# Packing the weight units and moving each low half behind its high half

## The chip, the cores and the metric

One NeuronCore of one Trainium2 chip runs the whole program. The metric is the device time of one execution in microseconds (us); of the kernel before three executions were timed, and their median is 2285.76 us (2285.3 to 2287.43).

## What is computed

A forward pass of 256 tokens of width 1024, in float32, through two blocks of two layers each. Cut to what carries the time:

```python
# first block, twice: layer norm, "0.5 * swiglu" with d_ff 4096, a mixer, and again a swiglu
x = layer_norm(alpha * x + 0.5 * swiglu(x, w_ff1_in, w_ff1_out), ...)     # (silu(gate) * up) @ w_out
x = layer_norm(alpha * x + hybrid_mixer(x, ...), ...)    # delta rule + two attentions, gates, w_out
x = layer_norm(alpha * x + 0.5 * swiglu(x, w_ff2_in, w_ff2_out), ...)
# second block, twice: a mixer (convolution and pooling; then sparse attention), and a swiglu, d_ff 2816
x = x + mixer(rms_norm(x, norm_mix))
x = x + swiglu_2(rms_norm(x, norm_ffn), ffn_gate, ffn_up, ffn_down)
```

Nearly all bytes and nearly all multiplications belong to products of the activations with weight matrices that are read once each.

## The kernel before

Each weight matrix is cut into *units* of at most 128 x 1040 numbers. There are 732 of them, taken in one fixed order. A unit goes through four steps, each on an engine of its own:

- SyncE loads it into one of four raw buffers `RW0` to `RW3` (`load`, L2316), which it may do once VectorE has finished with the unit four places earlier.
- ScalarE rounds it to the short format that TensorE multiplies fast and writes the *high half* `WH` (`cut`, L983; in the units marked `seven` L980 and L981).
- VectorE subtracts and writes the rest, the *low half* `WL` (`cut`, L1364; in `seven` units L1357 and L1360).
- TensorE multiplies. The activations are split in the same way (`XT` holds high and low in one row of 512 numbers, `HTH` and `HTL` are the hidden layer of a swiglu), and a product is the sum of three: high by high, high by low, low by high.

The program is written by a `Walk` that is run once for each engine; five `Program` classes issue the instructions of their engine and wait on semaphores. Order, waits and buffers come from the `Walk` and do not depend on addresses.

A pair (`WH[n]`, `WL[n]`) is a *slot*. There are six of them (`SPL = 6`); two more (`more_slots`, `WH6`, `WL6`, `WH7`, `WL7`) lie in the scratch area `SCR` and are lent for part of the time, and two (`xt_slots`) lie in `XT` itself, which is free while the second product of a large swiglu runs. A slot is placed by `Unit.place`, and `Unit.part` says where in it (and in the raw buffer) the unit's numbers lie. The forms of TensorE's work that the prediction speaks of are these:

- `tile_part` (L560, L559, L562): the gate and up products of a swiglu. The units are four blocks of 256 columns (nk = 4). The weights are the *stationary* operand, which is loaded into the array in its own instruction (PEld), and the activations stream through: for each block and column tile one matmul of 512 columns (high weights by high and low activations at once, L560), and one of 256 (low weights by high activations, L559; L562 in the first block).
- `rows_part` (L466, L467, L468, called through `mm3`): the down products and most projections. The units are two blocks of 512 columns (nk = 2). Activations are stationary, and the weights stream: `WH`, `WL`, `WH`, 512 columns each.
- `cols_part` (L463, L464, L465): some projections, with two blocks, weights stationary and 256 streaming columns.
- `seven_part` (L541, L542, L543): part of the down products, in matmuls of 256 columns, weights streaming.

In `Unit.part` a unit of more than two blocks lies packed at the front of its slot, 1024 numbers without a gap. A unit of one or two blocks keeps the slot's own rows, so its second block begins 520 numbers (2080 bytes) behind the first. In `XT` the rows are 512 numbers long, so a unit that is placed there has its second block 2048 bytes behind the first and its low half 4096 bytes behind its high half.

The tiles are given out one after the other in the order of the declarations. With distances counted in bytes from the start of `XT` (16384 bytes long) the raw buffers begin at 16384 and are 4160 bytes each, `WH[n]` begins at 33024 + 4160 n, `WL[n]` 24960 bytes behind `WH[n]`, then come `ST` (256 bytes) and the area `SCR` at 83200. All that lies in `SCR` (`HTH`, `HTL`, the lent slots, the mixers' tiles) is given by offsets from its start.

Of the kernel before, what the change touches and what calls it, by code (L numbers as in the profile page):

```python
# [11 lines left out]
R = mybir.dt.float32r  # L12

P = 128
# [8 lines left out]

KU = 2
UW = 520
RAW = 4
SPL = 6
LEAD = 4
# [103 lines left out]
class Signals:  # L132
# [15 lines left out]
    ]  # L148
    LOADS = (["d_raw%d" % n for n in range(RAW)] + ["d_x0", "d_x1", "d_ident", "d_const", "d_gb0", "d_gb1", "d_rg"]
             + ["d_small%d" % n for n in range(10)] + ["d_stage%d" % n for n in range(3)]  # L150
# [29 lines left out]
class Unit:  # L180
# [14 lines left out]
        self.h2, self.l2 = [v.rearrange("p k n -> p (k n)")[:, 0:768] for v in slot]  # L195

    def part(self, v):
        if self.nk <= KU:
            return v[:, 0:self.nk, 0:self.src.shape[2]]
        flat = v.rearrange("p k n -> p (k n)")  # L200
        return flat[:, 0:self.nk * self.src.shape[2]].rearrange("p (k n) -> p k n", k=self.nk)


class Tiles:


    def __init__(self, nc, a, ctx):
        self.a = a

        def sb(name, shape, dt=F):  # L210
            return ctx.enter_context(nc.sbuf_tensor(name, shape, dt))
# [6 lines left out]
        self.XT = sb("XT", [P, 8, 2 * T], R)  # L218
        self.XTH, self.XTL = self.XT[:, :, 0:T], self.XT[:, :, T:2 * T]
        self.RW = [sb(f"RW{n}", [P, KU, UW]) for n in range(RAW)]  # L220
        self.WH = [sb(f"WH{n}", [P, KU, UW], R) for n in range(SPL)]
        self.WL = [sb(f"WL{n}", [P, KU, UW], R) for n in range(SPL)]
        self.ST = sb("ST", [P, 64])
        self.PS = ctx.enter_context(nc.psum_tensor("PS", [P, 8, 512], F))
        room = 229344 - nc.sbuf_base - 96
# [6 lines left out]
        def at(kb, name, shape, dt=F):  # L232
            n = 4
            for s in shape[1:]:
                n *= s
            off = int(kb * K)
            assert off + n <= room, (name, off + n, room)
            tile = nc.alloc_sbuf_tensor_at(name, shape, dt, offset=base + off)
            return tile[tuple(slice(None) for _ in shape)]
# [8 lines left out]
        self.slots = [(self.WH[n], self.WL[n]) for n in range(SPL)]  # L248
        self.more_slots = [tuple(at(72 + 8.125 * n + 4.0625 * m, f"W{'HL'[m]}{SPL + n}", [P, KU, UW], R) for m in range(2))
                           for n in range(2)]  # L250
# [204 lines left out]
class TensorProgram(Program):  # L455
# [470 lines left out]
    def odd_out(self, I, b):  # L926
        k = self.k
        t = I.t
        self.wait_ge("odd_a", (I.id, "pt", t))
        self.wait_ge("odd_a", ("vv", 1))  # L930
        self.emptied(b)
        self.wait_ge("odd_a", ("vcb", 3))
        parts = [(x, kt) for x in range(2) for kt in range(t + 1)] + [None]
        for part, n in ([(part, n) for part in parts for n in range(2)] if t else
                        [(part, n) for n in range(2) for part in parts]):
            h = I.hs[n]
            if part is None:
                self.wait_ge("odd_a", "ptc")
                v, p = k.VCB[:, h // 2, h // 4, :], k.PTC[:, 2 * t + h % 2, :]
            else:  # L940
                v, p = k.VV[:, part[0], part[1], 64 * (h // 4):64 * (h // 4) + 64], I.pt[:, tsl(I.block(part[0], n, part[1]))]
            ins = self.e.matmul(I.out(b, n), v, p, start=part == (0, 0), stop=part is None, skip_group_check=True)
        ins.then_inc(*self.s["mm"].up(b.full))
# [18 lines left out]
class ScalarProgram(Program):  # L962
# [10 lines left out]
    def cut(self, u):  # L973
        k = self.k
        raw = u.part(k.RW[u.n % RAW])
        self.wait_ge(f"d_raw{u.n % RAW}", u.n)
        self.wait_each(u.after)
# [39 lines left out]
    def half_sum(self, f, seq, sl, n, part, j, b, free):  # L1017
        self.wait_each(free)
        self.wait_ge("mm", b.full)
        self.e.activation(f[2 + part][:, n, j * T:j * T + T], self.k.PS[:, b.n, 0:T],  # L1020
                          ACT.Copy).then_inc(*self.s["ffn_a"].up((seq, sl, n, part, j)))
# [305 lines left out]
class VectorProgram(Program):  # L1327
# [8 lines left out]
    def mix(self, u, mixed, free):  # L1336

        k = self.k
        raw = u.part(k.RW[u.n % RAW])
        b11, b12, b21, b22 = [raw[:, m, c] for m in range(2) for c in (slice(0, 256), slice(256, 512))]  # L1340
        t2, t3, t4 = [mixed[:, m, :] for m in range(3)]
        self.wait_ge(f"d_raw{u.n % RAW}", u.n)
        self.wait_each(free)
# [2199 lines left out]
```

## Time and profile before

| | |
|---|---|
| time, median of 3 | 2285.76 us (2285.3 to 2287.43) |
| the profiled execution, first to last instruction | 2283.4 us |
| TensorE matmuls, busy | 2250.3 us (99%), 14127 instructions |
| TensorE weight loads, busy | 1927.4 us (84%) |
| VectorE, busy | 1624.1 us (71%) |
| ScalarE, busy | 1193.1 us (52%) |
| GpSimd, busy | 128.4 us (6%) |
| DMA, mean rate | 179 GB/s |

The profile is of one execution. Times in its rows are us from the first instruction unless marked ns; a row `PS<-XT,WH` is an instruction that writes PSUM from the tiles XT and WH, the streaming and the stationary operand being named in no fixed order. Successive matmuls overlap, and the end of one is modelled, so the duration of a matmul is longer than the distance to the next one's start; both rise and fall together, since what one matmul takes longer delays the next start by as much.

### The profile page before, as it was taken

What the parts mean: (1) busy time and instruction counts of PE and PEld (TensorE: products, weight loads), DVE (VectorE), ACT (ScalarE), POOL (GpSimd) and SP (SyncE); (2) the same over time, 40 slices, a digit from 0 to 9 for tenths busy, and PEclk for the clock granted to TensorE, in tenths of its full rate; (3) what the DMA queues carried; (4) which work ended last, traced back from release to release, by engine and by line L of the source; (5) the groups of instructions that cost most, each with busy time, mean ns of one, the idle gap of its engine ahead of it and who ended that gap; (6) DMA issues with size and microseconds to landing.
All of it is one profiled execution on the core that took longest, in us unless ns stands there. A gap on an engine that the chain in (4) does not pass through costs nothing.

```text
span 2283.4 us, 34563 instructions
## 1 busy us (share of the span) xinstructions
PE 2250.3 (99%) x14127; PEld 1927.4 (84%) x14127; DVE 1624.1 (71%) x2491; ACT 1193.1 (52%) x1872; POOL 128.4 (6%) x185
## 2 busy tenths in 40 slices
PE   8999999999999999999999999999999999989999
PEld 7888899888888888888898877888878888867887
DVE  5777768857777777768668667776877778666776
ACT  5555446534555546555356444655444555545553
POOL 2100010120000000000100110000000000420000
PEclk9999999999999999999999999999999999999999
DMA  6765564435565556655554336665644666643654
GB/s 225 224 190 192 189 222 122 140 121 177 192 191 190 183 193 203 190 191 198 191 183 139 127 115 209 199 192 173 212 161 166 207 191 194 196 130 104 200 179 148
DMA packets 283567, 408.17 MB, mean 179 GB/s; under 512 B 13700, under 2 KB 170688, under 8 KB 283152
## 3 DMA queue, kind: packets, MB, share of 16 engines
q1 hardware_dynamic: 275600, 380.91, 51.9%
q0 software_dynamic: 7808, 25.04, 3.8%
q8 instruction: 112, 1.84, 0.3%
q14 instruction: 47, 0.39, 0.1%
HBM read 403.98 MB, written 1.91 MB: 178 GB/s over the span
## 4 chain that ended last, share of the span: by engine, by line
PE 89%; DVE 7%; ACT 3%; issue 1%; DMA 1%; SPq 0%; DVEq 0%; ACTq 0%
PE PS L560 24%; PE PS L466 12%; PE PS L468 12%; PE PS L467 12%; PE PS L559 11%; PE PS L463 2%; PE PS L465 2%; PE PS L464 2%; DVE WL L1364 2%; PE PS L562 2%; PE PS L483 1%; PE PS L543 1%; PE PS L541 1%; PE PS L542 1%; DVE QX L1659 1%
## 5 line engine op out<-in xcount | busy, mean ns | idle before, releaser
L1364 DVE TENSOR_TENSOR WL<-RW,WH 128x1024 fp32r<-128x1024 f32 x682 | 809.0, 1220 | 177.7 <-ACT WH L983 173.3
L560 PE MATMUL PS<-XT,WH 128*128 128x512 f32 x2368 | 808.0, 394 | 0.0
L983 ACT ACTIVATE WH<-RW 128x1024 fp32r<-128x1024 f32 x682 | 685.2, 1042 | 232.7 <-PE PS L468 62.9
L559 PE MATMUL PS<-XT,WL 128*128 128x256 f32 x2072 | 580.8, 280 | 0.0
L560 PEld LDWEIGHTS PS<-XT,WH 128*128 128x128 f32 x2368 | 425.2, 188 | 76.1
L559 PEld LDWEIGHTS PS<-XT,WL 128*128 128x128 f32 x2072 | 389.9, 188 | 13.4
L466 PE MATMUL PS<-WH,XT 128*128 128x512 f32 (+4 forms) x640 | 249.3, 390 | 3.8 <-DVE WL L1364 2.9
L468 PE MATMUL PS<-WH,XT 128*128 128x512 f32 (+4 forms) x640 | 240.5, 376 | 0.0
L467 PE MATMUL PS<-WL,XT 128*128 128x512 f32 (+4 forms) x640 | 240.0, 375 | 0.0
L466 PE MATMUL PS<-WH,HTH 128*128 128x512 f32 x488 | 192.6, 395 | 0.0
L468 PE MATMUL PS<-WH,HTL 128*128 128x512 f32 x488 | 192.2, 394 | 0.0
L467 PE MATMUL PS<-WL,HTH 128*128 128x512 f32 x488 | 191.4, 392 | 0.0
L463 PE MATMUL PS<-XT,WH 128*128 128x256 f32 x560 | 164.1, 293 | 2.3 <-DVE Z L1546 1.0
L464 PE MATMUL PS<-XT,WL 128*128 128x256 f32 x560 | 158.1, 282 | 0.0
L465 PE MATMUL PS<-XT,WH 128*128 128x256 f32 x560 | 158.1, 282 | 0.0
L1434 DVE TENSOR_TENSOR HM<-PS,HM 128x256 f32<-128x256 f32 x148 | 62.4, 422 | 133.1 <-ACT HM L1020 133.1
L466 PEld LDWEIGHTS PS<-WH,XT 128*128 128x128 f32 x640 | 121.2, 189 | 36.2 <-DVE XT L1375 8.6
L1020 ACT ACTIVATE HM<-PS 128x256 f32<-128x256 f32 x148 | 56.9, 384 | 169.6 <-PE PS L560 166.4
L468 PEld LDWEIGHTS PS<-WH,XT 128*128 128x128 f32 x640 | 121.1, 189 | 23.8
L467 PEld LDWEIGHTS PS<-WL,XT 128*128 128x128 f32 x640 | 121.4, 190 | 19.7
L1020 ACT ACTIVATE SG<-PS 128x256 f32<-128x256 f32 x148 | 54.2, 381 | 122.2 <-PE PS L560 120.8
L463 PEld LDWEIGHTS PS<-XT,WH 128*128 128x128 f32 x560 | 106.7, 190 | 6.9 <-issue 2.8
(500 smaller groups left out, 3221.8 us busy)
## 6 DMA issues: line engine op xcount, KB each, us to landing
RW<-in_w_ff_in SPq DMA_DIRECT2D x256, 512.0 KB, 4.4
RW<-in_w_ff_out SPq DMA_DIRECT2D x128, 512.0 KB, 4.5
RW<-in_w_in SPq DMA_DIRECT2D x56, 512.0 KB, 4.8
RW<-in_w_gate SPq DMA_DIRECT2D x48, 512.0 KB, 4.2
RW<-in_ffn_gate SPq DMA_DIRECT2D x44, 512.0 KB, 4.5
RW<-in_ffn_up SPq DMA_DIRECT2D x44, 512.0 KB, 4.7
RW<-in_ffn_down SPq DMA_DIRECT2D x44, 512.0 KB, 4.6
RW<-in_w_out SPq DMA_DIRECT2D x16, 512.0 KB, 4.8
```

Of the source, the lines that this page charges most:

```text
L463: self.e.matmul(o, wh, xh, start=start, stop=False)
L464: self.e.matmul(o, wl, xh, start=False, stop=False)
L465: return self.e.matmul(o, wh, xl, start=False, stop=stop)
L466: self.e.matmul(o, xh, wh, start=start, stop=False)
L467: self.e.matmul(o, xh, wl, start=False, stop=False)
L468: return self.e.matmul(o, xl, wh, start=False, stop=stop)
L559: self.e.matmul(k.PS[:, b.n, 0:T], wl, k.XTH[:, kt, :], start=False, stop=False)
L560: ins = self.e.matmul(k.PS[:, b.n, :], wh, k.XT[:, kt, :], start=kt == 0, stop=kt == 7)
L983: self.e.activation(u.hi_out, raw, ACT.Copy).then_inc(*self.s["hi"].up(u.n))
L1020: self.e.activation(f[2 + part][:, n, j * T:j * T + T], self.k.PS[:, b.n, 0:T], ACT.Copy).then_inc(*self.s["ffn_a"].up((seq, sl, n, part, j)))
L1364: self.e.tensor_tensor(u.lo_out, raw, u.hi_out.bitcast(F), ALU.subtract).then_inc(*self.s["lo"].up(u.n))
L1434: self.e.tensor_tensor(v, self.k.PS[:, b.n, T:2 * T], v, ALU.add).then_inc(*self.s["ffn_v"].up((seq, sl, n, part, j)))
```

## The change

`part` loses its special case, so that every unit lies packed at the front of its slot and of its raw buffer. The twelve tiles `WH0` to `WH5` and `WL0` to `WL5` become six tiles `W0` to `W5`, each of 1152 + 1040 numbers: the high half begins at 0, the low half at 1152 numbers, which is 4608 bytes. The slots' own shape stays two rows of 520.

```diff
 KU = 2
 UW = 520
+PAIR = 1152
@@ class Unit
     def part(self, v):
-        if self.nk <= KU:
-            return v[:, 0:self.nk, 0:self.src.shape[2]]
         flat = v.rearrange("p k n -> p (k n)")
         return flat[:, 0:self.nk * self.src.shape[2]].rearrange("p (k n) -> p k n", k=self.nk)
@@ class Tiles
         self.RW = [sb(f"RW{n}", [P, KU, UW]) for n in range(RAW)]
-        self.WH = [sb(f"WH{n}", [P, KU, UW], R) for n in range(SPL)]
-        self.WL = [sb(f"WL{n}", [P, KU, UW], R) for n in range(SPL)]
+        self.PAIRS = [sb(f"W{n}", [P, PAIR + KU * UW], R) for n in range(SPL)]
+        self.WH, self.WL = [[v[:, m * PAIR:m * PAIR + KU * UW].rearrange("p (k n) -> p k n", k=KU) for v in self.PAIRS] for m in range(2)]
```

A pair now takes 8768 bytes where it took 8320, so `WH[n]` begins at 33024 + 8768 n from the start of `XT`, `WL[n]` 4608 bytes behind it, and `SCR` with all that lies in it begins 2688 bytes further on, at 85888. No instruction is added or removed, and no wait, no order and no size is changed. The lent slots and those in `XT` keep their shape; a unit of two blocks is packed in the lent ones too.

## Rows read from the trace of the kernel before

**Rows 1.** The page: busy share, chain by engine, TensorE's granted clock, DMA share by slice
```profile
PE 2250.3 (99%) x14127; PEld 1927.4 (84%) x14127; DVE 1624.1 (71%) x2491; ACT 1193.1 (52%) x1872; POOL 128.4 (6%) x185
...
PEclk9999999999999999999999999999999999999999
DMA  6765564435565556655554336665644666643654
...
PE 89%; DVE 7%; ACT 3%; issue 1%; DMA 1%; SPq 0%; DVEq 0%; ACTq 0%
```

**Rows 2.** Stretches (swiglu in, swiglu down, mixer): busy us, clock, DMA share, GB/s
```profile
core 0: us, PE busy (x) PEld busy (x) DVE busy (x) ACT busy (x) POOL busy (x), PEclk, DMA share, GB/s
600.00:750.00 150.00, 150.00 (x863) 131.45 (x862) 106.43 (x155) 87.61 (x141) 0.00 (x0) 1.00 0.60 189
750.00:860.00 110.00, 109.95 (x556) 92.20 (x555) 84.29 (x116) 49.94 (x58) 1.05 (x2) 1.00 0.57 187
1070.00:1430.00 360.00, 357.88 (x2684) 305.98 (x2683) 255.63 (x420) 172.30 (x279) 31.32 (x33) 1.00 0.51 165
```

**Rows 3.** Groups by line and shape, TensorE: count, busy us, mean ns of one
```profile
L560 PE MATMUL PS<-XT,WH 128*128 128x512 f32 x2368 | 808.0, 394 | 0.0
L559 PE MATMUL PS<-XT,WL 128*128 128x256 f32 x2072 | 580.8, 280 | 0.0
L562 PE MATMUL PS<-XT,WL 128*128 128x256 f32 x296 | 82.7, 279 | 0.0
L466 PE MATMUL PS<-WH,HTH 128*128 128x512 f32 x488 | 192.6, 395 | 0.0
L468 PE MATMUL PS<-WH,HTL 128*128 128x512 f32 x488 | 192.2, 394 | 0.0
L467 PE MATMUL PS<-WL,HTH 128*128 128x512 f32 x488 | 191.4, 392 | 0.0
L467 PE MATMUL PS<-WL,XT 128*128 128x512 f32 x528 | 208.5, 395 | 0.0
L464 PE MATMUL PS<-XT,WL 128*128 128x256 f32 x560 | 158.1, 282 | 0.0
L466 PE MATMUL PS<-XT,HTH 128*128 128x512 f32 x72 | 28.1, 391 | 0.0
L468 PE MATMUL PS<-XT,HTL 128*128 128x512 f32 x72 | 28.1, 390 | 0.0
L467 PE MATMUL PS<-XT,HTH 128*128 128x512 f32 x72 | 28.0, 389 | 0.0
```

**Rows 4.** TensorE's instructions on tile XT: duration ns min/median/max, first and last start
```profile
L560 PE MATMUL PS<-XT,WH x2368: 387/394/486, 36.0 to 2219.4; 128*128 128x512 f32 x198
L559 PE MATMUL PS<-XT,WL x2072: 274/281/287, 36.4 to 2219.3; 128*128 128x256 f32 x189
L467 PE MATMUL PS<-XT,HTH x72: 387/389/396, 207.4 to 2262.3; 128*128 128x512 f32 x72
L543 PE MATMUL PS<-XT,HTL x40: 278/283/283, 210.2 to 2239.1; 128*128 128x256 f32 x40
L542 PE MATMUL PS<-XT,HSH x40: 278/283/283, 210.8 to 2240.0; 128*128 128x256 f32 x40
```

**Rows 5.** TensorE's instructions on tile WL: duration ns min/median/max
```profile
L467 PE MATMUL PS<-WL,HTH x488: 387/392/403, 193.8 to 2279.0; 128*128 128x512 f32 x163
L542 PE MATMUL PS<-WL,HTH x76: 276/281/284, 204.8 to 2257.1; 128*128 128x256 f32 x76
```

**Rows 6.** TensorE in order of time: start us, us; first and last of an even stretch
```profile
193.61 0.39 PE L466 MATMUL PS<-WH,HTH 128*128 128x512 f32 x1
...
199.85 0.39 PE L466 MATMUL PS<-WH,HTH 128*128 128x512 f32 x1
...
640.03 0.28 PE L559 MATMUL PS<-XT,WL 128*128 128x256 f32 x1
...
642.82 0.28 PE L559 MATMUL PS<-XT,WL 128*128 128x256 f32 x1
```

**Rows 7.** VectorE's low halves and ScalarE's high halves: duration ns min/median/max
```profile
L1364 DVE TENSOR_TENSOR XT<-RW,XT x18: 1214/1218/1228, 204.0 to 2252.2; 128x1024 fp32r<-128x1024 f32 x18
...
L1364 DVE TENSOR_TENSOR WL<-RW,WH x682: 682/1220/2318, 8.6 to 2264.6; 128x1024 fp32r<-128x1024 f32 x164, 128x512 fp32r<-128x512 f32 x4, 128x1040 fp32r<-128x1040 f32 x2, 128x560 fp32r<-128x560 f32 x1
...
L983 ACT ACTIVATE WH<-RW x682: 613/1052/1113, 7.6 to 2261.8; 128x1024 fp32r<-128x1024 f32 x164, 128x512 fp32r<-128x512 f32 x4, 128x1040 fp32r<-128x1040 f32 x2, 128x560 fp32r<-128x560 f32 x1
...
L983 ACT ACTIVATE XT<-RW x18: 1040/1045/1062, 200.8 to 2249.4; 128x1024 fp32r<-128x1024 f32 x18
```

**Rows 8.** Who waits for whom, us in total, times, longest; and loads with landing times
```profile
PE PS L466 <- DVE WL L1364: 2.9, 1, 2.9
...
PE PS L463 <- DVE WL L1364: 0.9, 1, 0.9
...
RW<-in_w_ff_in SPq DMA_DIRECT2D x256, 512.0 KB, 4.4
RW<-in_w_ff_out SPq DMA_DIRECT2D x128, 512.0 KB, 4.5
```

## The prediction, made before the changed kernel was run

> **What bounds the kernel now.** I read the page first: TensorE is busy for 99% of the span, it holds 89% of the chain that ended last, VectorE is busy 71% and ScalarE 52%, and the granted clock is in the top tenth (0.9 and more) in all forty slices [rows 1]. Then the stretches: in a swiglu's first product TensorE is busy in all 150.00 of 150 us and in its second in 109.95 of 110, at a granted clock of 1.00; in a mixer it is 357.88 of 360 [rows 2]. Next, who waits: on the low halves of the weights TensorE waits twice, 2.9 and 0.9 us [rows 8]. So the time is the number of matmuls times the pace of one. The change leaves the number alone. It can only move the time through the pace, or by making the preparation of weights so slow that TensorE waits.
>
> The pace is the interesting view. In the groups by shape the same form does not cost the same everywhere: streaming 512 columns against `HTH` or `HTL` takes 395, 392 and 394 ns (L466, L467, L468) when the weights lie in `WH` and `WL`, and 391, 389 and 390 when they lie in `XT` [rows 3]. Instructions, sizes, stationary operands and neighbours are the same; the place of the weights differs. The durations hold a modelled tail, so I checked the starts: 27 matmuls between 193.61 and 199.85 us are 231 ns each, and 8 pairs of L559 and L560 between 640.03 and 642.82 are 349 ns a pair [rows 6]. The medians say more than the means: in `XT` L467 has a minimum of 387 and a median of 389, so it sits at its floor, while in `WL` its median is 392 and it wanders up to 403; L560 goes from 387 with a median of 394 [rows 4, 5]. And the matmuls of 256 columns do the reverse: with weights in `XT` they sit at the top, median and maximum both 283, with weights in `WL` the median is 281, and L559 runs from 274 to 287 with a median of 281 [rows 4, 5]. I read this as a cost of some nanoseconds at the meeting of the two operand reads of TensorE, the streaming one and the weight load for the next matmul, which depends on addresses and settles where the addresses repeat.
>
> **What is special about `XT`.** Count addresses from `XT` and keep the remainder by 256 bytes (my choice: at 256 the six slots and the two halves sort themselves into few classes). In `XT` the halves lie 4096 apart and the blocks 2048, so every stream of a unit begins at remainder 0, and `HTH`, `HTL` too (83200 = 325 x 256). In the six slots the high half begins at 64 n (4160 = 16 x 256 + 64), the low half 128 further on (24960 = 97 x 256 + 128), and the second block 32 further on again (2080). So the remainder jumps at every matmul. After the change the low half is at the same remainder as the high half (4608 = 18 x 256), and so is the second block (2048). Within a unit nothing jumps any more, as in `XT`. What is not as in `XT` is the distance between the two operands: the slots stay at 64 n (8768 = 34 x 256 + 64), and `SCR` with `HTH` and `HTL` moves by 2688 = 10 x 256 + 128. Streaming against `HTH` the distance is 0 in slot 2 alone, against `XT` in slots 0 and 4. The rows show only distance 0 without jumps; the rest is a guess, and most of my width comes from it.
>
> **Part by part.**
>
> 1. *Streams of 512 columns* (L466 to L468, slots outside `XT`). Triples: 488 on `HTH`, 528 on `XT` [rows 3], and five groups of 32 on the mixers' outputs by the code, 1176. The price of a triple is 395 + 392 + 394 less 391 + 389 + 390, 11 ns. If all behave as in `XT` the gain is 1176 x 11 = 12.9 us. Bounds: 0, and 12.9. If they settle at a higher step than now (the maximum in `XT` is 396 against a mean near 394) they lose 2 ns each, 7.1 us.
>
> 2. *Gate and up* (L560 with L559 or L562, 2368 pairs). Nothing is packed here, those units were packed before; what changes is that the low half loses its 128. Bounds from the nearest rows: L560 from 394 to the 389 of `XT` gives 11.8 us; L559 and L562 from 280 to 283, as all matmuls of 256 do in `XT`, cost 7.1 us, or down to their own minimum of 274 they give 14.2 us. I take L560 at -4 and L559 at +1, near the `XT` rows but short of them since only two of six slots have distance 0: 2368 x 3 = 7.1 us gained.
>
> 3. *Other matmuls of 256 columns* (L463 to L465, 560 each; L541 to L543 outside `XT`, 144 each, together 2112). From 282 and 281 towards 283: I take +1 ns, 2.1 us lost. Bounds -6 and +2 ns: 12.7 us gained to 4.2 lost.
>
> 4. *VectorE and ScalarE.* A packed destination and source (`XT`) take 1218 and 1045 ns at the median, the slots 1220 and 1052 [rows 7]. The sign is a gain, under 1%. VectorE holds 7% of the chain, which is 160 us, and low halves are a part of that; 1% of it is 1.6 us at most. I take 0. Should it cost as much, the cover is that VectorE is busy only 106.43 of 150 us in the swiglu [rows 2].
>
> 5. *Loads.* The source rows stay apart, so a run is still 2048 bytes, and the gate and up units (packed, runs of 1024) land in 4.4 us where the down units (gapped, runs of 2048) land in 4.5 [rows 8]. The DMA share is 0.57 to 0.60 [rows 2]. I take 0; a load that lands 0.1 us earlier or later is hidden behind four raw buffers.
>
> 6. *Waits and order:* none is added or moved.
>
> Sum: 12.9 + 7.1 - 2.1 = 17.9 us off TensorE's work. In the swiglus all of it counts, and they hold all of point 2 and 488 of the triples; in the mixers TensorE leaves the chain at times, so I take 95% of the whole: 17 us. Against the profiled 2283.4 us that is 2266.4; the median of the runs is 2.4 us above that span, which gives 2269.
>
> **A rule against it.** The row: the same 512 columns take 392 from `WL` and 389 from `XT` [rows 4, 5]. The Trainium skill says otherwise, on the page "SBUF — State Buffer", section "Who interferes with whom": TensorE has two SBUF read ports, one for the streaming operand and one for weight loads, independent of each other, and TensorE and ScalarE never wait on anyone. By that rule no placement changes the pace and the sum is 0; this trace does not agree with its plain reading.
>
> **The rivals.**
>
> *Nothing moves, 2286 (2281 to 2290).* The difference between `XT` and the slots would be due to when those units run, not where they lie. They run only in the second product of a swiglu, between others, and are 72 triples of 1248. For it: the difference is 1%. Against it: the median sits on the floor in one form and on the ceiling in the other, which a mere share of idle neighbours wouldn't do. The section of the skill named above would give this outcome.
>
> *The floor everywhere, 2239 (under 2255).* If lack of jumps is all that matters, 512 columns go to 389 (12.9 + 11.8 us) and 256 columns near 275 (4480 x 5 = 22.4 us): 47 us, taken whole. Against it: the 283 of the 256-column forms in `XT`, where nothing jumps either.
>
> *Slower, 2297 (2291 to 2309).* With constant remainders each slot settles in one step for good, and at distances other than 0 that is no better than the present mixture. The place is the matmuls of 256 columns: L559 and L562 at 283 cost 7.1 us, the other 2112 at +2 cost 4.2, and the 512-column forms stay at 394: 11.3 us. It decides once the 256-column forms rise by 3 and the 512-column forms fall by less than 2 ns (5896 of them against 11.3 us). For it: the 283 rows. If the 512-column forms settle at 396 as well, another 12 us.
>
> *The change does less than it says:* packing touches only units of two blocks, and of 732 units 296 (gate and up) were packed. That is within point 2; if placement alone did nothing there, the gain is 10 us, 2276.
>
> **How the numbers follow.** Forecast, with the partial case (2255 to 2281): 0.46. Floor: 0.14. Nothing: 0.18. Slower: 0.22. A measurement of this kernel can tell about 0.2%, 4.6 us, from no change. Faster by more: 0.46 + 0.14 = 0.60; within: 0.18; slower: 0.22. The range leaves out the lower part of the floor case and the upper of the slower one: 2244 to 2298.
>
> **What would show it.** Right: in the changed profile L466 to L468 on `HTH` near 390 with a narrow spread, L560 at 390, L559 at 281, starts in the second product of a swiglu 227 to 228 ns apart where they were 231, VectorE and ScalarE at 1220 and 1050, no new wait of TensorE. Settled steps would show as medians equal to a minimum or a maximum. Wrong: L560 unchanged at 394 (then the low half's 128 was not the cause), L559 at 283 or above (slower rival), `HTH` forms unchanged with those on `XT` still at 389 (then distance 0 is what made `XT` fast, not the missing jumps). The prediction fails altogether if TensorE's pace is set by something other than addresses.

## The result and the profile after

The changed kernel takes 2290.52 us in the median (2288.79 to 2296.49, 17 runs), the kernel before 2285.39 us beside it (2282.64 to 2291.1, 17 runs). The ratio is 1.0024, with a 95% interval of 1.0018 to 1.003: slower by 0.24%, some 5 us, and just over what can be told from no change. I had forecast 2269. The sign is wrong, and the 17 us that I expected from TensorE's pace aren't there.

The page of the changed kernel, span 2288.1 us (before: 2283.4): busy shares, granted clock and the chain that ended last, as in [rows 1].

```profile
PE 2255.7 (99%) x14127; PEld 1929.4 (84%) x14127; DVE 1623.8 (71%) x2491; ACT 1193.5 (52%) x1872; POOL 128.4 (6%) x185
...
PEclk9999999999999999999999999999999999999999
...
PE 89%; DVE 7%; ACT 3%; issue 1%; DMA 1%; SPq 0%; DVEq 0%; ACTq 0%
```

TensorE's busy time grows by 5.4 us (2255.7 less 2250.3), the span by 4.7. VectorE, ScalarE, clock and chain stand where they stood. So the loss is TensorE's own. The same stretches as in [rows 2] (swiglu in, swiglu down, mixer), with busy us of each engine, clock, DMA share and GB/s:

```profile
600.00:750.00 150.00, 150.00 (x860) 131.07 (x859) 105.23 (x154) 86.87 (x139) 0.00 (x0) 1.00 0.60 190
750.00:860.00 110.00, 109.97 (x556) 92.02 (x556) 83.93 (x116) 51.01 (x61) 1.05 (x2) 1.00 0.55 183
1070.00:1430.00 360.00, 357.77 (x2680) 305.73 (x2679) 257.12 (x422) 172.96 (x279) 31.33 (x33) 1.00 0.51 164
```

TensorE is as full as before at the same clock of 1.00, and gets through 860 matmuls in the first stretch where it was 863. (The windows are fixed in time and the units come later by then, so the counts of the third stretch, 2680 and 2684, compare only roughly.) Now the groups by line and shape, which answer to [rows 3]. The lines are one lower than in the kernel before (L559 was L560), and the six slots are now called `W`; `WH` and `WL` are the lent slots alone; their rows are left out here.

```profile
L559 PE MATMUL PS<-XT,W 128*128 128x512 f32 x2232 | 765.5, 395 | 0.0
L558 PE MATMUL PS<-XT,W 128*128 128x256 f32 x1954 | 548.6, 281 | 0.0
L465 PE MATMUL PS<-W,HTH 128*128 128x512 f32 x440 | 174.1, 396 | 0.0
L466 PE MATMUL PS<-W,HTH 128*128 128x512 f32 x440 | 173.6, 395 | 0.0
L467 PE MATMUL PS<-W,HTL 128*128 128x512 f32 x440 | 173.5, 394 | 0.0
L463 PE MATMUL PS<-XT,W 128*128 128x256 f32 x536 | 151.8, 283 | 0.0
L561 PE MATMUL PS<-XT,W 128*128 128x256 f32 x278 | 78.5, 282 | 0.0
L465 PE MATMUL PS<-XT,HTH 128*128 128x512 f32 x72 | 28.4, 395 | 0.0
L466 PE MATMUL PS<-XT,HTH 128*128 128x512 f32 x72 | 28.5, 395 | 0.0
L467 PE MATMUL PS<-XT,HTL 128*128 128x512 f32 x72 | 28.4, 395 | 0.0
```

None of these rows went down. L465 to L467 on `HTH`, which I wanted at 391, 389 and 390, are at 396, 395 and 394. L561 rose from 279 to 282. And the last three rows are the ones that matter: the units in `XT`, whose own place and shape the change doesn't touch, lost their advantage. Min, median and max of one of them (before: 387/389/396, [rows 4]):

```profile
L466 PE MATMUL PS<-XT,HTH x72: 389/394/405, 207.3 to 2267.0; 128*128 128x512 f32 x72
```

The only thing about them that moved is `HTH`, by 2688 bytes, of which 128 are left over 256.

The waits (engine that waits, and for whom; us in total, times, longest) are those of [rows 8]:

```profile
PE PS L465 <- DVE W L1363: 2.9, 1, 2.9
...
PE PS L462 <- DVE W L1363: 0.8, 1, 0.8
```

### The profile page after: what moved, and what is told of

It reads as the page before. It is cut to its first block, busy times and chain, and to the rows that moved or that the text cites. A ratio compares the mean times of both kernels' runs of the same rounds, so it can differ in the third digit from the quotient of the medians.

```text
span 2288.1 us, 34563 instructions
## 1 busy us (share of the span) xinstructions
PE 2255.7 (99%) x14127; PEld 1929.4 (84%) x14127; DVE 1623.8 (71%) x2491; ACT 1193.5 (52%) x1872; POOL 128.4 (6%) x185
## 4 chain that ended last, share of the span: by engine, by line
PE 89%; DVE 7%; ACT 3%; issue 1%; DMA 1%; SPq 0%; DVEq 0%; ACTq 0%
PE PS L559 24%; PE PS L465 12%; PE PS L467 12%; PE PS L466 12%; PE PS L558 11%; PE PS L462 2%; PE PS L464 2%; PE PS L463 2%; DVE W L1363 2%; PE PS L561 2%; PE PS L482 1%; PE PS L540 1%; PE PS L542 1%; PE PS L541 1%; DVE QX L1658 1%
## 5 line engine op out<-in xcount | busy, mean ns | idle before, releaser
L1363 DVE TENSOR_TENSOR W<-RW,W 128x1024 fp32r<-128x1024 f32 (+1 forms) x631 | 749.1, 1219 | 154.5 <-ACT W L982 151.3
L559 PE MATMUL PS<-XT,W 128*128 128x512 f32 x2232 | 765.5, 395 | 0.0
L982 ACT ACTIVATE W<-RW 128x1024 fp32r<-128x1024 f32 (+1 forms) x631 | 634.3, 1041 | 193.1 <-PE PS L467 60.8
L558 PE MATMUL PS<-XT,W 128*128 128x256 f32 x1954 | 548.6, 281 | 0.0
L559 PEld LDWEIGHTS PS<-XT,W 128*128 128x128 f32 x2232 | 402.2, 188 | 74.8
L558 PEld LDWEIGHTS PS<-XT,W 128*128 128x128 f32 x1954 | 368.0, 188 | 12.0
L465 PE MATMUL PS<-W,XT 128*128 128x512 f32 (+3 forms) x580 | 224.6, 387 | 3.7 <-DVE W L1363 2.9
L467 PE MATMUL PS<-W,XT 128*128 128x512 f32 (+3 forms) x580 | 216.9, 374 | 0.0
L466 PE MATMUL PS<-W,XT 128*128 128x512 f32 (+3 forms) x580 | 216.7, 374 | 0.0
L465 PE MATMUL PS<-W,HTH 128*128 128x512 f32 x440 | 174.1, 396 | 0.0
L466 PE MATMUL PS<-W,HTH 128*128 128x512 f32 x440 | 173.6, 395 | 0.0
L467 PE MATMUL PS<-W,HTL 128*128 128x512 f32 x440 | 173.5, 394 | 0.0
L462 PE MATMUL PS<-XT,W 128*128 128x256 f32 x536 | 157.3, 293 | 1.7 <-DVE Z L1545 0.9
L463 PE MATMUL PS<-XT,W 128*128 128x256 f32 x536 | 151.8, 283 | 0.0
L464 PE MATMUL PS<-XT,W 128*128 128x256 f32 x536 | 151.7, 283 | 0.0
L465 PEld LDWEIGHTS PS<-W,XT 128*128 128x128 f32 x580 | 109.7, 189 | 32.7 <-DVE XT L1374 6.7
L467 PEld LDWEIGHTS PS<-W,XT 128*128 128x128 f32 x580 | 109.9, 190 | 21.0
L466 PEld LDWEIGHTS PS<-W,XT 128*128 128x128 f32 x580 | 110.1, 190 | 17.3
L462 PEld LDWEIGHTS PS<-XT,W 128*128 128x128 f32 x536 | 102.8, 192 | 6.1 <-issue 2.8
```

What stands on the lines that cost most here:

```text
L462: self.e.matmul(o, wh, xh, start=start, stop=False)
L463: self.e.matmul(o, wl, xh, start=False, stop=False)
L464: return self.e.matmul(o, wh, xl, start=False, stop=stop)
L465: self.e.matmul(o, xh, wh, start=start, stop=False)
L466: self.e.matmul(o, xh, wl, start=False, stop=False)
L467: return self.e.matmul(o, xl, wh, start=False, stop=stop)
```

## The experiments

### A measure that all kernels share

Durations in the rows hold a modelled tail; what adds up to the span is the distance from one matmul's start to the next one's. I took its mean from the starts in each trace, for each line (without distances over 16 ns off the usual 231 or 115, which hold waits; they are few but for L466 and L468, where 9 and 6 in a hundred are left out). The lines are numbered as before the change. The first three columns are gate and up (2368, 2072 and 296 matmuls), the next three are the streams of 512 columns of `rows_part`, those of the mixers included (1248 each), L464 is the middle one of the three in `cols_part`. "Low" and "SCR" are what is left by 256 bytes of the distance from high half to low half, and of the place of the scratch area with `HTH`.

```
kernel           low SCR  blocks  L560   L559   L562   L466   L467   L468   L464   span
before           128   0  gapped  231.8  117.4  116.9  232.1  230.0  231.6  117.8  2283.4
before_shifted   128 128  gapped  231.7  117.4  117.0  232.6  231.0  232.2  118.0  2285.8
pack_only        128   0  packed  231.7  117.5  116.9  231.5  230.4  230.8  117.5  2281.8
near_128_gap     128   0  packed  231.8  117.5  116.8  231.4  230.5  230.7  117.6  2280.3
near_128         128 128  packed  231.7  117.4  116.9  231.9  230.8  231.3  117.4  2282.1
changed            0 128  packed  232.5  117.7  119.4  232.3  231.9  231.9  117.9  2288.1
changed_gap128     0   0  packed  232.5  117.8  119.2  232.2  230.9  231.3  118.0  2289.0
place_only         0 128  gapped  232.5  117.8  119.2  232.5  231.9  232.7  118.2  2287.7
far_same           0 128  gapped  232.5  117.8  119.2  232.5  231.8  232.7  118.2  2288.7
all_zero           0   0  packed  233.8  116.1  115.1  228.2  228.3  228.4  119.7  2280.7
```

In `all_zero` the slots, too, all begin at 0; in the nine others they begin at 64 n. The experiments below fill this table row by row. The span is that of the one profiled execution. Executions of the kernel before lie between 2282.64 and 2291.1 us, so spans that differ by 2 or 3 us are no evidence by themselves; the medians of 8 to 25 executions and the starts are.

### TensorE alone, and beside its neighbours

`micro_streams` is a kernel of its own: streams of matmuls at chosen addresses, first with TensorE alone, then the same beside VectorE's subtractions, beside ScalarE's rounding, and beside loads.

```diff
+            for j, (dl, dk) in enumerate(((0, 2048), (64, 2048), (128, 2048), (128, 2080))):
+                for d in range(4):
...
+                    for i in range(N_ROWS // 3):
+                        slot, kk = i // 2 % 4, i % 2
+                        h = M0 + 4352 * 2 * slot + kk * dk + 64 * d
+                        lo = h + 4352 + dl
+                        s = S0 + 1024 * (i % 8)
+                        ops += [(s, h, 512), (s, lo, 512), (s + 8192, h, 512)]
```

`dl` is the remainder by which the low half lies further on, `dk` the distance of the second block; each triple is (stationary, streaming, columns). "Distance" is from here on the address of the streaming operand less that of the stationary one, by its remainder by 256; in gate and up, where the weights are stationary, the micro kernels count from the activations to the high weights.

> A kernel of its own, no forward pass: TensorE runs stretches of 24 to 32 matmuls whose addresses are chosen, first alone (A), then beside VectorE subtractions (V), beside ScalarE copies (C), beside loads of 512 KB (D). In each of them 16 stretches stream 512 columns in the order high, low, high of a down product (distance of the streaming from the stationary operand 0, 64, 128 or 192 bytes modulo 256; the low half displaced by 0, 64 or 128, and in a fourth set the second block by 2080 in place of 2048), 8 alternate 256 and 512 columns as the gate and up products do, 8 stream 256 columns only. Theory J (jumps of the remainder): the stretches without displacement run at the floor, 389 ns a matmul of 512 columns, those with it at 392 to 394, at every distance. Theory D (distance): distance 0 at 389 and the others at 392 to 396, jump or no jump. Theory N (neighbours): alone, every stretch is at one pace, near 389 and 275, whatever the addresses, and the spread comes back beside VectorE, ScalarE or the loads, whichever of them shares the memory with TensorE.

Measured: 692.95 us. The engines' busy time in parts of the four sections (alone; VectorE; ScalarE; loads):

```profile
30.00:190.00 160.00, 160.00 (x849) 136.97 (x848) 0.00 (x0) 0.00 (x0) 0.00 (x0) 1.00 0.00 1
196.00:356.00 160.00, 160.00 (x849) 137.00 (x848) 145.69 (x129) 0.00 (x0) 0.00 (x0) 1.00 0.00 1
362.00:500.00 138.00, 138.00 (x667) 115.13 (x666) 0.00 (x0) 138.00 (x146) 0.00 (x0) 1.00 0.00 1
530.00:560.00 30.00, 30.00 (x132) 24.39 (x131) 0.00 (x0) 0.00 (x0) 0.00 (x0) 1.00 1.03 382
```

160 us hold 849 matmuls with VectorE idle, and 849 with VectorE busy for 145.69 us. The same stream in each of the four sections, at a distance of 0 between stationary and streaming operand, then at 128 (line: min/median/max in ns):

```profile
L153 PE MATMUL PS<-WTS,ACTS x24: 389/389/389, 33.6 to 38.9; 128*128 128x512 f32 x24
L221 PE MATMUL PS<-WTS,ACTS x24: 389/389/389, 199.2 to 204.4; 128*128 128x512 f32 x24
L289 PE MATMUL PS<-WTS,ACTS x24: 389/389/389, 364.7 to 369.9; 128*128 128x512 f32 x24
L357 PE MATMUL PS<-WTS,ACTS x24: 389/389/389, 530.2 to 535.4; 128*128 128x512 f32 x24
L157 PE MATMUL PS<-WTS,ACTS x24: 390/394/404, 44.6 to 50.0; 128*128 128x512 f32 x24
L225 PE MATMUL PS<-WTS,ACTS x24: 390/394/404, 210.1 to 215.5; 128*128 128x512 f32 x24
L293 PE MATMUL PS<-WTS,ACTS x24: 390/394/404, 375.6 to 381.0; 128*128 128x512 f32 x24
L361 PE MATMUL PS<-WTS,ACTS x24: 390/394/404, 541.2 to 546.5; 128*128 128x512 f32 x24
```

Two things follow. The neighbours don't matter: the means of each stream agree within 0.2 ns in all four sections, even with loads at 382 GB/s beside it. (VectorE's work ends at 342 us and ScalarE's at 501, a little before their sections do; all streams of 512 columns had them beside.) And in neither of these streams does the remainder jump from one half, or one block, to the next; only the distance to the stationary operand differs. 389 is what `XT` showed, 394 with 404 at the top what `WL` showed [rows 4, 5]. In starts, behind the first few and good to about 1 ns, without jumps: 226.7 ns at distance 0, 229.0 at 64, 232.4 at 128, 233.3 at 192. With the layout before (low half 128 further on, second block 2080): 231.5, 232.3, 231.3, 232.6. So "no jumps" is worth 4.8 ns at distance 0, 3.3 at 64, and costs 1.1 and 0.7 at 128 and 192. A pair of gate and up (256 and 512 columns) takes 353.8, 352.4, 350.5 and 351.8 ns at the four distances with the low half at +0, and 349.7, 352.0, 351.7 and 346.7 at +128. The six slots begin at 0, 64, 128, 192, 0 and 64; their mean is 352.5 without the 128 and 350.3 with it. This predicts a loss: 2.2 ns for each of 2368 pairs, 5.2 us. The whole kernel lost less there, 3.0 us, and the scan further down, which follows the kernel's own order of addresses, puts the two layouts only 0.5 ns a pair apart (350.4 and 350.9 over the six places). The sign held, the size didn't.

### The parts of the change

The kernel before with nothing but the scratch area moved by 2688 bytes:

```diff
         self.ST = sb("ST", [P, 64])
+        sb("GAP", [P, 672])
```

> The kernel before with a gap of 2688 bytes ahead of the scratch area, so that HTH, HTL and all else in it lie where the change puts them, and the weights as before. Theory D: the down units in XT lose their 389 and go to 394 as in the changed kernel, and the time rises by a part of the 5 us. Theory J: they stay at 389, no difference in time. Theory N: no telling difference in either, or a scatter of one or two us.

Measured: 2286.75 us beside 2285.12, ratio 1.0006 (0.9997 to 1.0015). The time can't be told from no change, but the rows show one. The middle line of the triple in `XT` (L467 of the kernel before, where it was 387/389/396) is now

```profile
L468 PE MATMUL PS<-XT,HTH x72: 390/393/405, 207.4 to 2264.7; 128*128 128x512 f32 x72
```

Nothing but the scratch area moved, so the distance to `HTH` alone took the `XT` rows from 389 to 393. Their matmuls of 256 columns left the top in the same run: L543 on `HTL` had 278/283/283 and has 274/282/288.

The changed kernel with the special case of `part` put back, so that only the placement of the halves differs from before:

```diff
     def part(self, v):
+        if self.nk <= KU:
+            return v[:, 0:self.nk, 0:self.src.shape[2]]
```

> The change without the packing: pairs of 8768 bytes with the low half 4608 bytes behind the high half, units of two blocks keep the gap of 2080. Theory J: the second block's jump stays, so the down units do not gain, gate and up as in the changed kernel; 2288 to 2291. Theory D: as the changed kernel within 2 us, since the distances are the same. Theory N: anything within 3 us of the changed kernel.

Measured: 2290.95 us beside 2285.12, ratio 1.0026 (1.0015 to 1.0036).

The kernel before with the packing alone, the same two lines taken away:

```diff
     def part(self, v):
-        if self.nk <= KU:
-            return v[:, 0:self.nk, 0:self.src.shape[2]]
```

> The change without the new placement: units packed, WH and WL and the scratch area where they were. Theory J: between before and 2 us faster. Theory D: XT units stay at 389, gate and up as before (L560 at 394), so within 2 us of before. If it is as slow as the changed kernel (+5 us), packing is the cause and the placement is not.

Measured: 2286.39 us beside 2285.12, ratio 1.0001 (0.9992 to 1.0009).

So the placement is the whole loss, and the packing is worth nothing that the times can tell. In the table packing takes 0.6 and 0.8 ns off L466 and L468 and adds 0.4 to L467: 1.0 ns of a triple, 1.2 us for 1248 triples. That is what is left of my 11 ns a triple. Moving the scratch area adds 0.5, 1.0 and 0.6 ns there, 2.1 ns a triple, 2.6 us; the medians show 1.6 us, which their interval doesn't tell from none.

### One pair of addresses over and over, and a scan

`simple_streams` repeats one pair of addresses twelve times, alone on the core, and then hops one of the two. `scan_streams` runs the kernel's own orders for each place of the high half and each offset of the low half, in steps of 32 bytes.

```diff
+            for x, y, w, st, sp in run([(43456,76512,512),(43456,76512,512), ...
+                e.matmul(ps[:, 1, 0:w], x, y, start=st, stop=sp)  # same 512 distance 32
...
+            for x, y, w, st, sp in run([(43456,76480,512),(43584,76480,512),(43456,76480,512), ...
+                e.matmul(ps[:, 1, 0:w], x, y, start=st, stop=sp)  # stationary hops 128 distance 0
```

(The lists are cut. Each entry is stationary, streaming, columns; 43456 is the place of `XT`, and 76480, 33024 bytes behind it, that of the weights.)

> TensorE alone, no forward pass: stretches in which the same two addresses, or two addresses in turn, are used by every matmul. It asks what the pace depends on. If the distance of the two operands modulo 256 bytes is all that counts, the stretches at distances 1024, 2048 and so on are alike, moving both by the same amount changes nothing, and hops of a multiple of 256 cost nothing. If the absolute place or higher address bits count, these differ by up to 6 to 13 ns a matmul.

> TensorE alone with the real sequences of addresses of a gate-and-up pair of units, of a down pair against HTH and HTL, and of a projection against XT, for 8 places of the high half (steps of 32 bytes modulo 256) and 8 (projection 4) of the low half. The first scan of streams gave 346.7 to 353.8 ns for a pair of L559 and L560 and 226.7 to 233.8 for 512 columns. If the pace is a sum over addresses, the present placements (low half +128 before, +0 after) come out some 2 ns a pair apart in favour of before, and some other place lies below both, by up to 6 ns a pair.

Measured: 403.52 and 933.04 us. Four streams of 512 columns (min/median/max ns): distance 0, distance 128, distance 256, and distance 0 with the stationary operand hopping by 128 at every matmul.

```profile
L61 PE MATMUL PS<-WTS,XT x12: 389/389/389, 34.6 to 37.1; 128*128 128x512 f32 x12
```
```profile
L69 PE MATMUL PS<-WTS,XT x12: 392/394/398, 45.7 to 48.3; 128*128 128x512 f32 x12
```
```profile
L77 PE MATMUL PS<-WTS,XT x12: 389/389/395, 56.9 to 59.4; 128*128 128x512 f32 x12
```
```profile
L203 PE MATMUL PS<-WTS,XT x14: 396/396/397, 217.6 to 220.6; 128*128 128x512 f32 x14
```

In starts, means of the last nine distances of each stretch (good to about 1 ns, for some were still settling): 226.7 ns at distance 0, 233.6 at 32, 228.9 at 64, 234.6 at 96, 233.9 at 128, 233.6 at 160, 233.6 at 192, 232.2 at 224, and again from the start at 256. (The third row is not quite that: L77 is the group at 256, and its maximum of 395 is what it takes to settle after the group before.) At the fourteen multiples of 1024 from 2048 to 15360 it is 226.7 each time (at 1024, which came first after other addresses, 230.2, still settling), and 128 beyond a multiple it is 233.8 or 233.9 in all fifteen. Moving both operands by 32, 512 or 1024 bytes leaves 226.7; moved by 64, 96 or 128 the stretch takes some seven matmuls to come back to it, and moved by 192 or 256 it gets there with the last. So what it settles at goes by the distance and not by the place. Hops of either operand by 256 and its multiples cost nothing at distance 0 once the pace has settled. A stationary operand that hops by 128 makes 233.3 of 226.7. A streaming one that hops by 128, as the prediction's jump between high and low half does, makes some 230, and some 230 of the 233.9 at distance 128 too: halfway between the two distances that it visits, with no cost of the jump itself to be seen. For 256 columns the order is another one: 119.6 ns at distance 0, and 113.8, the lowest, at 192. That settles what I had wondered at in [rows 4]: in `XT` the 512-column form sits at its floor and the 256-column form at its top for the same reason, the distance 0; `before_shifted` shows both leaving it together.

The scan gave no placement of the low half that is better throughout. For a gate and up pair the best was the high half at 192 and the low half 64 further, 343.9 ns against 350.1 with everything at 0; but streaming against `XT` the same slot takes 234.5 ns instead of 226.9. Weighted with the kernel's counts of those three forms, everything at 0 came out first among layouts in which all slots have the same place; `cols_part` and `seven_part` weren't in the scan.

### Everything at 0, and the scratch area back

`all_zero`: the changed kernel with slots 8704 bytes apart (34 x 256) and low halves 4352 behind (17 x 256), so that `XT`, the scratch area and the six slots with both halves are multiples of 256 apart (the lent slots keep their own shape, with halves 4160 bytes apart).

```diff
-PAIR = 1152
+PAIR = 1088
-        self.PAIRS = [sb(f"W{n}", [P, PAIR + KU * UW], R) for n in range(SPL)]
+        self.PAIRS = [sb(f"W{n}", [P, 2 * PAIR], R) for n in range(SPL)]
```

> The change with pairs of 8704 bytes and the low half 4352 behind the high half, so that XT, all six slots, both halves and the scratch area have the same remainder by 256. The prediction's theory J: the floor for 512 columns, some 25 us faster than before. By the first scan: down and projection triples at 226.7 a matmul, that is 12 to 14 us gained, and gate and up at 353.8 ns a pair against 350.3 before, 8 us lost: 2279 to 2283. Theory of no effect of addresses: 2285.

Measured: 2282.11 us beside 2284.54, ratio 0.9983 (0.9974 to 0.9991). It is faster than both kernels: by the ratios 0.17% under the one before and 0.4% under the changed one.

```profile
L559 PE MATMUL PS<-XT,W 128*128 128x512 f32 x2232 | 765.4, 396 | 0.0
L558 PE MATMUL PS<-XT,W 128*128 128x256 f32 x1954 | 545.0, 279 | 0.0
...
L465 PE MATMUL PS<-W,HTH 128*128 128x512 f32 x440 | 171.9, 391 | 0.0
L466 PE MATMUL PS<-W,HTH 128*128 128x512 f32 x440 | 171.5, 390 | 0.0
L467 PE MATMUL PS<-W,HTL 128*128 128x512 f32 x440 | 171.3, 389 | 0.0
L462 PE MATMUL PS<-XT,W 128*128 128x256 f32 x536 | 157.3, 293 | 4.2 <-DVE W L1363 3.1 <-DVE Z L1545 1.1
```

Here are the 391, 390 and 389 that I had forecast for the change. In starts a triple falls from 693.7 to 684.9 ns, 8.8 ns by 1248 triples, 11.0 us. What is given back: `cols_part` rises by 1.7 ns (1680 x 1.7 = 2.9 us), `seven_part` by a good 1 ns (672, 0.8 us), gate and up by 1.3 us in sum (+2.0 ns by 2368, -1.3 by 2072, -1.8 by 296), and the last row shows TensorE waiting 3.1 us at L462 for a low half, where it was 0.9 [rows 8]. Left are some 4 us; the span is 2.7 shorter and the median 2.4.

`changed_gap128`: the changed kernel with `HTH` at remainder 0 again.

```diff
         self.ST = sb("ST", [P, 64])
+        sb("GAP", [P, 32])
```

> The changed kernel with a gap of 128 bytes ahead of the scratch area, so that HTH and HTL are back at remainder 0 from XT. By distances: the down units in XT are back at 389 ns, the other down units a little faster (the six slots now stand at 0, 64, 128, 192, 0, 64 from HTH in place of 128, 192, 0, 64, 128, 192), together 2 to 4 us faster than the changed kernel, 2286 to 2289. If the placement of the scratch area has no part: 2290.5.

Measured: 2289.2 us beside 2284.54, ratio 1.0018 (1.0009 to 1.0027), span 2289.0. That is at the slow edge of what was expected, and 1.3 us under the changed kernel where 2 to 4 were expected; the two can't be told apart by their times.

```profile
L467 PE MATMUL PS<-XT,HTH x72: 387/389/397, 208.0 to 2267.9; 128*128 128x512 f32 x72
```

The `XT` units are back at 389, though nothing about them was touched but the distance to `HTH`. They are 72 triples, so that alone is 1 us. In the table the whole triple falls by 1.7 ns against the changed kernel, 2.1 us; gate and up stay where they were.

### Is it the remainder, or that the halves lie close together?

The changed kernel also moves the halves from 24960 to 4608 bytes apart. Three kernels separate nearness from the remainder. `far_same` is the kernel before, with the halves as far apart as ever but at the same remainder:

```diff
         self.WH = [sb(f"WH{n}", [P, KU, UW], R) for n in range(SPL)]
+        sb("GAP", [P, 32])
         self.WL = [sb(f"WL{n}", [P, KU, UW], R) for n in range(SPL)]
```

> The kernel before with 128 bytes of nothing between the six high tiles and the six low ones: the low half of each slot then lies 25088 bytes behind its high half (98 x 256, at the same remainder by 256, as in the changed kernel), yet as far away as before, and HTH and HTL move by 128 bytes to the remainder that they have in the changed kernel. Blocks keep their gap of 32 bytes. Theory (only the remainder by 256 of the distances between TensorE's two operands counts): the loss of the changed kernel, without its compact slots: ratio 1.002 to 1.003, 2289 to 2291. Rival (the loss comes from the two halves lying close together, 4608 bytes apart, or from the slot pitch of 8768): no difference from before, 2284 to 2287.

Measured: 2291.44 us beside 2285.26, ratio 1.0029 (1.0018 to 1.0039). 128 unused bytes in the kernel before make the whole loss.

`near_128` is the changed kernel with the low half 4736 bytes behind in place of 4608, slots still 64 n apart:

```diff
-PAIR = 1152
+PAIR = 1184
-        self.PAIRS = [sb(f"W{n}", [P, PAIR + KU * UW], R) for n in range(SPL)]
+        self.PAIRS = [sb(f"W{n}", [P, 2256], R) for n in range(SPL)]
```

> The changed kernel with compact slots, but the low half 4736 bytes behind the high half (18 x 256 + 128) in place of 4608, and slots 9024 bytes apart (64 n by 256, as in both kernels). HTH and HTL stay at the changed kernel's remainder of 128. Remainder theory: the gate and up pairs get back what they had before, about 1.3 ns of a pair, 3 us; with HTH at 128 this is the shifted kernel before, ratio 1.0006: 2285 to 2288. Rival (nearness): as the changed kernel, 2289 to 2291.

Measured: 2284.75 us beside 2285.26, ratio 0.9998 (0.9989 to 1.0006). The loss is gone. L561 is back at 279, and the row in `XT` stays at 395, since `HTH` stays at 128:

```profile
L559 PE MATMUL PS<-XT,W 128*128 128x512 f32 x2232 | 763.1, 394 | 0.0
L558 PE MATMUL PS<-XT,W 128*128 128x256 f32 x1954 | 547.8, 280 | 0.0
...
L463 PE MATMUL PS<-XT,W 128*128 128x256 f32 x536 | 150.5, 281 | 0.0
L464 PE MATMUL PS<-XT,W 128*128 128x256 f32 x536 | 150.5, 281 | 0.0
L561 PE MATMUL PS<-XT,W 128*128 128x256 f32 x278 | 77.6, 279 | 0.0
...
L465 PE MATMUL PS<-XT,HTH 128*128 128x512 f32 x72 | 28.4, 395 | 0.0
```

And `near_128_gap` is the same with `GAP` of 32 numbers ahead of the scratch area, so that all remainders but those of packed blocks are the ones of the kernel before:

```diff
         self.ST = sb("ST", [P, 64])
+        sb("GAP", [P, 32])
```

> As the kernel with the low half 4736 bytes behind and slots 9024 bytes apart, with 128 bytes of nothing ahead of the scratch area, so that HTH and HTL are at remainder 0 too: every remainder by 256 is that of the kernel before, but for packed second blocks (which were worth nothing). Remainder theory: the time of the kernel before, ratio 0.9995 to 1.0007, 2284 to 2287. Rival (nearness): 2289 to 2291.

Measured: 2282.72 us beside 2285.26, ratio 0.9991 (0.9983 to 1.0), a little faster than was expected of it. It is also within 1 us of `all_zero`, in the median (2282.11) as in the span (2280.3 and 2280.7), and their intervals overlap: everything at 0 is the fastest in the streams of 512 columns, but the times don't show that it beats this layout with its slots at 64 n.

Nearness plays no part that these runs can tell. In the table `far_same` and `place_only` agree within 0.1 ns in every column, one with its halves 25088 bytes apart and the other with 4608; `near_128_gap` and `pack_only` agree within 0.1 likewise. The five kernels with the low half at +128 have L560 at 231.7 or 231.8 and L562 at 116.8 to 117.0, the four with +0 and slots at 64 n have 232.5 and 119.2 to 119.4.

## Why the prediction was wrong, point by point

*What bounds the kernel.* Right. TensorE's pace is all that the change moves: busy share, clock, chain, waits and loads stood still, and points 4, 5 and 6 of the sum held at 0 (low halves at a median of 1219 ns on `W` for 1220, the units of the swiglus' first and second product landing in 4.4 and 4.5 us as before). That the pace depends on addresses and settles where they repeat was right as well.

*What is special about `XT`.* This is the step that failed. Two things set `XT` apart, no jumps of the remainder and distance 0 from the stationary operand. I had named both, saw that the change brings only the first, and priced the rows as if the first were most of it. The streams of one repeated pair of addresses have no jump at all and still take 233.9 ns at distance 128 against 226.7 at 0. I had even written down the row that would tell ("`HTH` forms unchanged with those on `XT` still at 389, then distance 0 is what made `XT` fast"); what came was the stronger form of it: the `XT` rows went to 394 themselves, since `HTH` had moved. One reading of the kernel before was off too. The remainder does not jump at every matmul: L468 and the next triple's L466 both stream `WH`, so it jumps at two of three.

*Point 1, triples, -12.9 us.* Wrong in size and sign. In starts the change adds 0.2, 1.9 and 0.3 ns to L466, L467 and L468, 2.4 ns a triple, 3.0 us for 1248. Taken one at a time in the table, the moved scratch area adds 2.1 ns, packing takes 1.0 off, and the low half at +0 adds 1.3 (`before_shifted` to `far_same`) to 2.2 (`near_128` to the change). The term of 11 ns a triple is what measured +2.4. The 72 triples in `XT`, which the sum left out as untouched, lost some 5 ns a matmul, 1 us of these 3.

*Point 2, gate and up, -7.1 us.* Wrong sign. L560 rose by 0.7 to 0.8 ns (2368, 1.8 us), L559 by 0.2 (2072, 0.5 us), L562 by 2.5 (296, 0.7 us): 3.0 us lost, 1.3 ns a pair. (The separate streams had said 2.2.) My price of -4 for L560 was the row of another form (L467 on `HTH` in `XT`) with another order, 512 columns after 512. L560 comes after 256 columns, and the row for that order at distance 0 is no faster: 233.8 in `all_zero`, where everything is at 0.

*Point 3, other 256 columns, +2.1 us.* Nearly nothing: L464 rose by 0.1.

The sum by starts closes with what the table leaves out. From the kernel before to the changed one, the distances that the table is made of add 3.0 us in gate and up, 3.2 in `rows_part` and 0.6 in `cols_part`; all else between TensorE's starts (the mixers' small matmuls, and the distances left out above) takes 350.4 us for 352.4, 2.0 less. Together that is the 4.7 us of the span. This remainder, from 346.4 in `place_only` to 356.7 in `all_zero`, is also why the spans follow the table only roughly; what moves it is not traced.

By kernels, in medians, it reads: moving the scratch area costs 1.6 us with the low halves at +128 (`before_shifted` against the kernel before beside it) and 2.0 between `near_128_gap` and `near_128`; the low halves at +0 cost 4.7 between `before_shifted` and `far_same` and 5.8 between `near_128` and the change. The low halves are the larger part. With them at +0, moving the scratch area back gives 1.3 us. The costs of 1.3 to 2.0 us are each within the noise of the times, and rest on the table.

*The rivals.* The slower one, at 0.22, has the sign: each slot settles, and at distances other than 0 that is no better than the mixture. Its size was too large (2291 to 2309), since it put L559 at 283 when it stayed at 281, and only L562, one in eight of these, rose by 3; 2290.5 is just outside its edge. "Nothing moves" is wrong by the interval, if barely. "The floor everywhere" fell with the first step. That the range, 2244 to 2298, held the time is owed to the slower rival and says nothing for the forecast.

*The rule against it.* In the four sections of the streams TensorE paid nothing for its neighbours, with VectorE, ScalarE or loads at work (GpSimd was not tried). So the Trainium skill, page "SBUF — State Buffer", section "Who interferes with whom", is right that TensorE never waits on anyone there. Its other statement, that the two read ports of TensorE are independent of each other, doesn't hold to the last 3% in its plain reading: the same stream takes 226.7 or 233.9 ns with the addresses of its two operands as the only difference, and moving both together leaves 226.7. Where in the chip the two reads meet, no run here shows. I had taken the gap between rule and row as support for my reading; it supports any reading by addresses, mine and the right one.

What stays open: why 32, 96, 128, 160 and 192 are worse than 64 for 512 columns and 192 best for 256, and why the same distance can settle in two paces (233.9 at 128 and 232.2 at 640 bytes, whose remainder by 256 is 128 too). The history of the stream matters, and I have no model that gives a pace from a list of addresses.

## What to carry to other kernels

When one group of rows is faster than its siblings, list every property that sets it apart, and price the change by those that it brings; if it brings only one of two, the rows don't carry the price. Where tiles move, look also at what lies behind them: here `HTH` moved with the slots, and the fastest rows of the kernel lost their pace though nothing of theirs was edited. For a kernel that is all TensorE, the placement was worth between -0.17% and +0.29% here. All distances at multiples of 256 gave the best streams of 512 columns, but it cost those of 256 columns in `cols_part` and `seven_part`, and another layout came to the same time; 128 bytes of padding did as much harm as the whole change.

## What the runs showed of the hardware

- A matmul of 512 columns whose weights are loaded anew each time takes 226.7 to 234.6 ns from start to start at the granted clock of 1.00, by the distance from its stationary to its streaming operand modulo 256 bytes (one address pair repeated, `simple_streams`); one of 256 columns takes 113.8 to 119.6, with its best and worst elsewhere (192 and 0). Beside VectorE at work for 145.69 of 160 us, beside ScalarE for 138 of 138, and beside loads at 382 GB/s the pace is the same.
- Hops of either operand by 256 bytes and its multiples cost nothing at distance 0 once settled; a stationary operand that hops by 128 costs 6.6 ns of 226.7. A streaming one that hops between the distances 0 and 128 takes some 230, halfway between their paces.
- After a change of addresses the pace takes up to some ten matmuls to settle (230.2 ns on average at 1024 bytes after other addresses, 226.7 at the next fourteen multiples), and the same remainder can settle in two cycles (233.9 and 232.2 ns).
